# Two VectorE jobs moved in a hybrid decoder step, and smaller blocks in the products of a gated recurrence

## The reference: what is computed

```python
for l in range(DEPTH):
    xp, ... = _layer(xp, 0, None, None, None, lbs[l], *lw)                      # the prompt
    xs, ... = _layer(xs, PAST_LEN, past, state_win[l], state_hgrn[l], lbs[l], *lw)   # the 8 new tokens
```

```python
b = jnp.cumsum(gc, axis=2)
diff = b[:, :, :, None, :] - b[:, :, None, :, :]
decay = jnp.exp(jnp.where(tril[:, :, None], diff, -jnp.inf))
A = jnp.einsum('bhtk,bhsk,bhtsk->bhts', qc, kc, decay)
```

```python
score = jnp.where(kpos[None, None, :] <= qp[None, :, None], score, NEG)
sel = lax.top_k(score, n_top)[1]
```

## Time and profile before

| what | value |
|---|---|
| time, median of 3 runs | 991.56 us (988.15, 992.10, 991.56) |
| the profiled execution | 992.23 us, its span 990.6 us |
| PE busy | 952.4 us (96%) |
| VectorE busy | 480.5 us (49%) |
| ACT busy | 303.4 us (31%) |
| POOL busy | 132.4 us (13%) |
| DMA | 188.96 MB, mean 191 GB/s |

### The profile page before, as it was taken

The page is one execution under the profiler, slowest core; times in us unless marked ns, Lnnn a source line. Parts: engine busy times, 40 slices in busy tenths (PEclk is TensorE's granted clock), DMA queues, the critical chain, the costliest instruction groups (busy, mean ns, idle before and its releaser), DMA issues.

```text
span 990.6 us, 16671 instructions
## 1 busy us (share of the span) xinstructions
PE 952.4 (96%) x6058; PEld 775.3 (78%) x6058; DVE 480.5 (49%) x1350; ACT 303.4 (31%) x657; POOL 132.4 (13%) x258
## 2 busy tenths in 40 slices
PE   8999998999999999999999999899999999899998
PEld 6888777987677777888888886698777767678887
DVE  4223588778656403124240345887786463041331
ACT  2135422236743113310121463222476321133000
POOL 0510000002023261000060000000020413600000
PEclk9999998999999999999999999999999999999999
DMA  7644417435279798334454434274341997952432
GB/s 260 201 159 167 156 49 294 171 121 194 80 242 381 251 386 286 114 128 160 138 186 135 148 137 163 111 278 147 139 171 43 352 361 267 380 204 89 169 128 87
DMA packets 56212, 188.96 MB, mean 191 GB/s; under 512 B 9154, under 2 KB 22850, under 8 KB 43586
## 3 DMA queue, kind: packets, MB, share of 16 engines
q1 hardware_dynamic: 42850, 138.56, 40.0%
q0 software_dynamic: 12992, 49.16, 13.1%
q10 hardware_dynamic: 288, 0.18, 0.1%
HBM read 177.47 MB, written 18.77 MB: 198 GB/s over the span
## 4 chain that ended last, share of the span: by engine, by line
PE 83%; DVE 6%; ACT 4%; DVEq 2%; DMA 2%; issue 2%; ACTq 1%; SPq 1%
PE ps L883 24%; PE ps L999 16%; PE ps L1335 9%; PE ps L1343 6%; PE ps L1228 5%; PE ps L1027 3%; PE ps L872 2%; PE ps L1306 2%; DMA arena<-in_win_k_dram 2%; PE ps L1139 2%; PE ps L1127 2%; PE ps L1207 1%; DVE top L1796 1%; PE ps L1107 1%; DVEq L1799 1%
## 5 line engine op out<-in xcount | busy, mean ns | idle before, releaser
L883 PE MATMUL ps<-hT,slab 128*128 128x264 f32 (+1 forms) x1184 | 273.5, 390 | 0.0
L883 PEld LDWEIGHTS ps<-hT,slab 128*128 128x128 f32 (+1 forms) x1184 | 225.8, 193 | 39.7 <-issue 2.4
L999 PE MATMUL ps<-hT,slab 128*128 128x264 f32 x768 | 179.6, 391 | 1.7 <-DVEq L2092 1.7
L999 PEld LDWEIGHTS ps<-hT,slab 128*128 128x128 f32 x768 | 143.7, 191 | 32.7 <-issue 3.3
L1355 ACT ACTIVATE arena<-ps 128x512 f32<-128x512 f32 (+21 forms) x152 | 69.7, 484 | 179.7 <-PE ps L883 70.1
L1335 PE MATMUL ps<-Y,slab 128*128 128x264 f32 x384 | 85.8, 387 | 0.0
L1335 PEld LDWEIGHTS ps<-Y,slab 128*128 128x128 f32 x384 | 73.2, 191 | 12.3
L1228 PEld LDWEIGHTS ps<-arena,w 128*128 128x128 f32 x512 | 58.4, 192 | 10.0 <-issue 6.6
L1747 DVE SCALAR_TENSOR_TENSOR arena<-arena,small 128x264 f32<-128x264 f32 x26 | 11.0, 488 | 110.7 <-ACT arena L1430 110.7
L1228 PE MATMUL ps<-arena,w 128*128 128x128 f32 x512 | 61.4, 279 | 0.0
L1343 PE MATMUL ps<-arena,slab 128*128 128x264 f32 x256 | 57.5, 387 | 2.3 <-DVEq L2232 2.3
(11 more groups left out here) (360 smaller groups left out, 1184.4 us busy)
## 6 DMA issues: line engine op xcount, KB each, us to landing
slab<-in_weights_dram SPq DMA_DIRECT2D x86, 1024.0 KB, 4.9
arena<-in_pages_kv_dram SPq DMA_DIRECT2D x64, 256.0 KB, 8.5
arena<-in_pages_kv_dram POOLq DMA_DIRECT2D x64, 256.0 KB, 6.6
arena<-in_pages_kv_dram POOLq DMA_DIRECT2D x64, 128.0 KB, 7.3
arena<-in_pages_kv_dram SPq DMA_DIRECT2D x64, 128.0 KB, 11.3
out_dram<-in_state_win_dram POOLq DMA_DIRECT2D x2, 4088.0 KB, 25.8
arena<-in_state_hgrn_dram SPq DMA_DIRECT2D x2, 2048.0 KB, 7.6
out_dram<-arena POOLq DMA_DIRECT2D x2, 2048.0 KB, 6.8
```

The source lines that it names most:

```text
L883: last = mm(ps[0:job[3], n % 2, 0:LT], v[:, k, job[2]:job[2] + job[3]], hT[:, k, :], start=(k == 0), stop=(k == KD - 1))
L999: last = mm(ps[:, bank, 0:LT], v[:, k, (d % 2) * 128:(d % 2) * 128 + 128], hT[:, k, :], start=(k == 0), stop=(k == KD - 1))
```

## The change

Three edits, in both layers.

1. On VectorE `top_keys` (both parts) and the mask move from around `f` to after the levels, just ahead of the wait for `qk` on PE.
2. The 32 rounds of `left_out` move back: four rounds leave the levels, 14 rounds ahead of `qk` and five after it are now four rounds after it; nine rounds stay in the compression of the prompt (with other numbers), and the last 19, the ranking and the marks stand in the page stage, between the joins.
3. On PE the products of levels 0 to 6 run only over blocks in which the mask can keep something: for levels 0 to 4 the two 64x64 blocks on the diagonal, for level 5 two blocks of 32 keys by 32 queries, for level 6 one of 64 by 64. VectorE's merge copies the same or somewhat larger areas: four copies of 64 partitions instead of two of 128 for levels 0 to 5, two of 64 partitions for level 6.

```diff
+                def level_blocks(i):
+                    if i < 5:
+                        return [(h, h) for h in halves]
+                    if i == 5:
+                        return [(slice(r, r + 32), slice(r + 32, r + 64)) for r in (0, 64)]
+                    return [(halves[0], halves[1])]
...
                             for h in range(4):
-                                x = m[:, h, t * 128:t * 128 + 128]
-                                last = mm(ps[:, b + t, h * 128:h * 128 + 128], x, x, start=True, stop=True)
+                                for s, q in level_blocks(i):
+                                    x = m[:, h, t * 128 + s.start:t * 128 + s.stop]
+                                    y = m[:, h, t * 128 + q.start:t * 128 + q.stop]
+                                    last = mm(ps[s, b + t, h * 128 + q.start:h * 128 + q.stop], x, y, start=True, stop=True)
...
-                top_keys(slice(0, 128))
-
                 ve.wait_ge(hg_a.sem, hg_a(l, "gates"))
...
                 ve.drain().then_inc(hg_v.sem, hg_v.mark("f"))
-                top_keys(slice(128, 384))
-                TS(msk, acc, taken, NEG, ALU.not_equal, ALU.mult)
-                ve.drain()
-                TT(msk, msk, causal, ALU.add)
-                ve.drain().then_inc(pidx_v.sem, pidx_v.mark("mask"))
...
+                    if i < 0:
+                        areas = [(slice(0, 128), slice(0, 128))]
+                    elif i < 6:
+                        areas = [(h, h) for h in halves]
+                    else:
+                        areas = [halves]
                     for t in range(2):
-                        nc.vector.copy_predicated(AT[:, t, :, :], lvl[:, level:level + 1, :].to_broadcast([128, 4, 128]),
-                                                  ps[:, banks + t, :].rearrange("p (h t) -> p h t", h=4))
+                        for s, q in areas:
+                            w = q.stop - q.start
+                            nc.vector.copy_predicated(AT[s, t, :, q], lvl[s, level:level + 1, q].to_broadcast([s.stop - s.start, 4, w]),
+                                                      ps[s, banks + t, :].rearrange("p (h t) -> p h t", h=4)[:, :, q])
...
-                    if 2 <= i <= 5:
-                        left_out([i - 2])
...
-                left_out(range(4, 18))
+                top_keys(slice(0, 128))
+                top_keys(slice(128, 384))
+                TS(msk, acc, taken, NEG, ALU.not_equal, ALU.mult)
+                ve.drain()
+                TT(msk, msk, causal, ALU.add)
+                ve.drain().then_inc(pidx_v.sem, pidx_v.mark("mask"))
                 ve.wait_ge(hg_p.sem, hg_p(l, "qk"))
...
-                left_out(range(18, 23))
+                left_out(range(0, 4))
...
-                left_out(range(23, 32))
+                left_out(range(4, 13))
...
-                best_of_pairs()
-                sort_pairs()
-                threshold()
                 ve.wait_ge(cp_p.sem, cp_p(l, "o"))
...
+                left_out(range(13, 18))
+                join(0)
+                left_out(range(18, 28))
+                join(1)
+                left_out(range(28, 32))
+                best_of_pairs()
+                join(2)
+                sort_pairs()
+                threshold()
                 for step in range(4):
                     compared(step)
                 for step in range(7):
                     limits(step)
                 for step in range(3):
                     dropped_ties(step)
-                for p in range(NPAIR):
-                    join(p)
+                join(3)
```

## The result

The changed kernel takes 983.28 us (median of 5 runs, 981.35 to 988.15) against 991.22 beside it; the ratio is 0.9926 [0.9899, 0.9954]. It is faster, by 8 us and not by the 20 of the forecast: 971 was 12 too low, and 983.28 lies above the range. In a second set of eight runs it took 985.14 against 993.88 (0.9926 again).

A forecast was written before the change was run, and what follows sets the result against it. PE, busy for 952.4 us, was taken as the bound. From the profiled 992.23 us, less 14.8 (Term 1) and 8.2 (Term 2), plus 2.0 (Term 3), came 971.2, given as 971 us; range 965 to 981.

The forecast's parts named there:

- Term 1: Between `a diag` and level 1: moving the selection ends PE's wait for `flat` and the slow clock; 7.4 us less per layer.
- Term 2: Levels 0 to 6: smaller products on PE, with VectorE's merges still covered, save 4.1 us in each layer.
- rival B: Levels: loads of the two column halves do not overlap, 1.9 us lost per layer, 983 us; chance 0.1.
- cover of 0.4 us: Levels: VectorE's step of 4.4 us stays below PE's 4.8, so PE does not wait for merges.
- rival C: Levels: small copies cost 0.72 us each, so VectorE sets the pace; 6.6 us per layer, 984 us; chance 0.08.
- Term 3: Page stage, where the moved VectorE work goes: PE waits for the marks, 2.0 us more in layer 0, nothing in layer 1.
- nothing in layer 1: Page stage, layer 1: marks ready at 866.0, before PE needs them at 867.0, with the 2.57 us window-key wait kept.
- Rival A: Behind the marks in layer 0: the clock falls after 3.4 us idle, +1.8 to +2.7 us, 974 us; chance 0.2.
- faster: Whole kernel: a time below 986.6 us, held by the forecast, A, B, C and half of E; chance 0.92.

The follow-up runs named there:

- before_fill: Kernel before the change plus nine useless matmuls in PE's wait ahead of the products of `flat`; 987.9 us, ratio 0.9947 to the kernel before.
- pace: win_early with the merges of levels 1, 3 and 5 made by two full copies instead of four small ones; 976.3 us, ratio 0.9840 to before.
- win_late: Changed kernel with the 4 MB window copy issued some 50 us later, after the chunks' final state; 991.5 us, ratio 0.9986 to before.
- win_early: Changed kernel with the 4 MB window copy issued some 22 us earlier, behind the second index-key product; 978.1 us, ratio 0.9852 to before.
- after_again: Changed kernel rerun as it is, for more runs and a second profile; 985.1 us, ratio 0.9926 to before.
- win_early_2: win_early rerun unchanged as a measure on the same chip; 982.8 us, ratio 0.9910 to before.
- filled_6: win_early plus six useless matmuls on PE ahead of its wait for the marks; 971.5 us, ratio 0.9812 to before.
- after_fill: Changed kernel plus six useless matmuls on PE ahead of its wait for the marks; 981.1 us, ratio 0.9878 to before.

## Why the prediction was wrong

**Term 1** held. From `a diag` to level 1 it is 7.36 us (7.8 forecast; with the smaller level 0, 7.3), `flat` does not wait, level 0 is at 2.4 GHz, and before_fill shows the clock's share.

**Term 2** was right in PE's part and wrong in what goes with it. A level takes 1.09 us (levels 0 to 4) and 0.63 (level 5), the changes of form 0.2; in all some 4 us against 4.1. The page "TensorE: Matmul & The Clock Gate" of the Trainium skill, "Part 3: Packing small matmuls — row/col tiling", has a weight load overlap a running product only where the two use different rows, and here all use the same 128. The trace does not agree: 32 records in 1.09 us, 34 ns each, half of L1269's 67, say that the two column halves overlap, and rival B falls. But the merges were mis-sized: a copy over half the partitions and half the columns (a quarter of the elements, where I wrote half) takes 0.45 us from start to start, where a full one took 0.63; 1.82 for a merge where I took 1.45. VectorE's step is 4.87 against PE's 4.84, so the cover of 0.4 us is not there. `m 6` is late by 0.26, and `m 7` by 1.4, since VectorE has no lead left when the longer differences come; pace, with the cheaper merges at three levels, has 0 and 0.16. I had rival C either in full or not at all; it came at a quarter of its size (1.64 of 6.6 in a layer) and was hidden by the slab.

**What no step priced.** This is the step that failed first: the sum has no term for DMAs. Term 1 moved two PE steps, and two DMAs hang on them. The prediction followed PE, VectorE and ACT and left SP and POOL aside. The state's load and the 4 MB copy came 6 and 8.6 us earlier and met: 2.58 and 3.11 us of waiting for a slab, 1.8 for the clock behind the second. win_late and win_early move only the copy, and the wait goes; win_early shows too that only 2.1 to 3.6 of it were to be had without a faster merge. No run moves the state's load, so whether the copy would have held up the slabs without it stays open.

**Term 3.** In layer 0 the marks cost 1.7 net, 2.0 forecast. In layer 1 I let the 2.57 us for window keys stand as cover; it went to 0.3, and the marks' wait took its place, 3.58 (2.2 net): no loss against the forecast, by luck. My reading "nothing in layer 1" failed. The wait for window keys is no fixed term: it was 1.9 us in layer 0 of after_again and 1.0 in layer 1 of win_early_2; what sets it no run shows.

**Rival A**, chance 0.2, came in both layers: from the marks to L1246 it is 5.99 and 6.80 us, where filled_6 at full clock has 4.35, so 1.6 and 2.4 us in the profile, and win_early, with a longer fall, loses 3.3 and 3.2. It should have been part of the forecast. The earlier trace rows showed 0.50 after 4.5 us of idle time, and the new wait has 3.4; the evidence that I set against it was one wait of 2.57 us.

The sum for the profiled run: 971.2, slab 5.7 and its clock 1.8, `m 6` 0.5, clock at the marks 4.1, three half-clock stretches at places where before had none (278, 766, 797 us) with 6.4, less 1.6 for the one at 115 us that before had and this run has not: 988.1, measured 988.15. Without those at other places it is 983.3, and the median is 983.28; but no median run was profiled, and after_again's profile has other falls, so how near the two come is partly luck. Why the clock falls at such places, where PE has hardly any idle time, stays open: they come and go between runs of one kernel, and neither fill nor order explains them.

The chances that the prediction adds up for "faster" give 0.95 and not 0.92; nothing hangs on it.

## What to carry to other kernels

When a step moves, list the transfers that wait for it and ask which other transfer they will now meet; an issue that is bound to a compute step only by habit can go where the DMA engines are idle. If PE's work shrinks beside another engine's, make that engine's step from the measured price of the new shape: a copy of half the columns in half the partitions cost 0.72 of a full one here. Judge small gains by span times granted clock, unless they are gains of the clock, and before a long wait is accepted, see what its clock costs: a fill of useless products that ends inside the wait gave some 5 us here in after_fill and before_fill, by the ratios.

## What I had not expected of the hardware

- Products of 64 columns of weights, alternating between the two column halves, cost 34 ns each (32 in 1.09 us), and of 32 columns 20 ns (32 in 0.63).
- A masked copy of 64 x 256 takes 0.45 us from start to start, one of 128 x 512 0.63.
- Six products without use in a 3.6 us wait, twice in the program, took a kernel from between 978 and 983 us down to 971.5.
- The runs of one kernel spread over 11 us (988 to 999) with mean clocks from 0.988 to 0.978, while time by clock had a standard deviation of 1.2.
